# Two edits in a two-layer kernel: an empty interleaving step, and a table stored in one hop

## The reference, cut to what matters

```python
proj = h @ w_in[l]
(cb, cc, cv, q, k, v, qm, ga, gb, gc) = jnp.split(proj, IN_OFFSETS, axis=-1)
y_a = (cb * causal_dwconv(cc * cv, conv_mix_w[l])) @ w_conv_out[l]
o = moba_attention(to_heads(q), to_heads(k), to_heads(v), rel_bias)
y_b = jnp.transpose(o, (0, 2, 1, 3)).reshape(b_, s_, ATT_W) @ w_attn_out[l]
y_c = memory_attention(qm, rmsnorm(mem, g_mem[l]), w_mem_kv[l]) @ w_mem_out[l]

# in moba_attention, for the keys of a query's own block (and likewise for the earlier block):
s_own = jnp.einsum("bhqd,bhkd->bhqk", qc, ko).astype(jnp.float32) * scale
bias_own = bias_hb[:, rel_bucket(dist)]
s_own = jnp.where(dist[None, None] >= 0, s_own + bias_own[None], NEG)
```

## Time and profile before

| what | value |
|---|---|
| median of 3 runs | 2201.85 us (2200.92 to 2204.42) |
| profiled execution, its own time | 2201.85 us |
| its span (first to last instruction) | 2199.8 us |
| PE busy | 2022.4 us, 92% of the span |
| DVE, ACT, POOL busy | 993.9, 702.0, 218.5 us |
| chain that ended last | PE 70%, DMA 16%, DVE 8% |

### The profile page before, as it was taken

The page is one execution under the profiler, slowest core; times in us unless marked ns, Lnnn a source line. Parts: engine busy times, 40 slices in busy tenths (PEclk is TensorE's granted clock), DMA queues, the critical chain, the costliest instruction groups (busy, mean ns, idle before and its releaser), DMA issues.

```text
span 2199.8 us, 23022 instructions
## 1 busy us (share of the span) xinstructions
PE 2022.4 (92%) x9514; PEld 1407.9 (64%) x9514; DVE 993.9 (45%) x1558; ACT 702.0 (32%) x1122; POOL 218.5 (10%) x281
## 2 busy tenths in 40 slices
PE   7999999997999999889999999999995988888887
PEld 6767788896888788777777765666693332332232
DVE  4466524426666522677888436652235111111113
ACT  4343422324444312554555323552121110100100
POOL 2000000002000000001111002110023111111110
PEclk9999999998999999999999999999996999999999
DMA  7331122242222322232222221112229999999995
GB/s 259 106 112 61 67 87 96 97 153 105 97 96 96 134 96 86 100 136 90 74 96 101 87 95 58 58 58 77 77 106 376 414 423 423 424 422 422 417 411 225
DMA packets 56856, 380.43 MB, mean 173 GB/s; under 512 B 12936, under 2 KB 13192, under 8 KB 23856
## 3 DMA queue, kind: packets, MB, share of 16 engines
q1 hardware_dynamic: 38304, 339.23, 39.5%
q0 software_dynamic: 17872, 38.68, 5.0%
q10 hardware_dynamic: 576, 1.05, 0.1%
HBM read 378.82 MB, written 27.89 MB: 185 GB/s over the span
## 4 chain that ended last, share of the span: by engine, by line
PE 70%; DMA 16%; DVE 8%; ACT 3%; issue 1%; POOL 1%; SPq 0%; DVEq 0%; POOLq 0%; ACTq 0%
PE PS L490 17%; PE PS L491 16%; PE PS L492 16%; DMA AR<-in_wexp 15%; PE PS L1071 5%; PE PS L864 4%; PE PS L537 2%; DVE AR L1331 2%; DVE rf L1113 2%; ACT rf L1928 1%; PE PS L845 1%; PE PS L1094 1%; PE PS L486 1%; PE PS L897 1%; PE PS L929 1%
## 5 line engine op out<-in xcount | busy, mean ns | idle before, releaser
L490 PE MATMUL PS<-rf,rf 128*128 128x512 f32 (+1 forms) x1896 | 725.2, 382 | 22.9 <-DVE rf L1113 16.0
L491 PE MATMUL PS<-rf,rf 128*128 128x512 f32 (+1 forms) x1896 | 712.4, 376 | 0.0
L492 PE MATMUL PS<-rf,rf 128*128 128x512 f32 (+1 forms) x1896 | 711.5, 375 | 0.0
L1113 DVE TENSOR_TENSOR rf<-AR,rf 128x1024 fp32r<-128x1024 f32 (+1 forms) x210 | 268.4, 1285 | 385.1 <-ACT rf L1928 384.8
L490 PEld LDWEIGHTS PS<-rf,rf 128*128 128x128 f32 x1896 | 360.1, 190 | 97.6 <-issue 22.7
L492 PEld LDWEIGHTS PS<-rf,rf 128*128 128x128 f32 x1896 | 360.1, 190 | 64.8
L491 PEld LDWEIGHTS PS<-rf,rf 128*128 128x128 f32 x1896 | 360.3, 190 | 64.2 <-issue 3.1
L1928 ACT ACTIVATE rf<-AR 128x1024 fp32r<-128x1024 f32 (+1 forms) x210 | 229.1, 1101 | 304.4 <-PE PS L492 210.1
L1071 PE MATMUL PS<-AR 128*64 128x512 f32 x1024 | 271.7, 639 | 51.9 <-DMA AR<-in_wexp 50.8
L1071 PEld LDWEIGHTS PS<-AR 128*64 128x64 f32 x1024 | 84.2, 147 | 233.6 <-issue 159.8
L1873 DVE TENSOR_TENSOR AR<-AR,PS 128x256 f32<-128x256 f32 x32 | 13.5, 421 | 360.3 <-ACT AR L2370 360.3
(11 more groups left out here) (326 smaller groups left out, 1830.4 us busy)
## 6 DMA issues: line engine op xcount, KB each, us to landing
AR<-in_wexp SPq DMA_DIRECT2D x62, 2048.0 KB, 35.9
AR<-in_wpack SPq DMA_DIRECT2D x123, 1024.0 KB, 5.1
AR<-in_wexp SPq DMA_DIRECT2D x68, 1024.0 KB, 38.1
AR<-acud POOLq DMA_DIRECT2D x16, 512.0 KB, 4.1
AR<-ya SPq DMA_DIRECT2D x4, 1024.0 KB, 7.9
bvec<-bv POOLq DMA_DIRECT2D x1, 2560.0 KB, 16.3
AR<-in_x SPq DMA_DIRECT2D x4, 512.0 KB, 7.4
AR<-bvec POOLq DMA_DIRECT2D x8, 256.0 KB, 3.0
```

Of the source, the lines that this page charges most:

```text
L490: e.i.matmul(o, ws[0], xs[0], start=start, stop=False)
L491: e.i.matmul(o, ws[0], xs[1], start=False, stop=False)
L492: return e.i.matmul(o, ws[1], xs[0], start=False, stop=stop)
L1113: e.i.tensor_tensor(rounded(p.place + p.width, p.width), src, rounded(p.place, p.width).bitcast(F32), ALU.subtract).then_inc(*tick("w_lo", ...
```

## The change

There are two edits.

**1.** In `attention_1` of PE, DVE and ACT one of the two yields after the first pair of heads goes. All later steps of the attention then stand one dense step earlier among the dense work. POOL and SP have no such generators.

**2.** `bv8` goes, with its store and POOL's wait for it. One DMA now writes `bvec` straight from SBUF: its source is the 8 partitions of BV, each read 128 times, its destination `bvec` in order.

```diff
--- before.py
+++ after.py
@@ -601,7 +601,6 @@
 
 
                 scores(0)
-                yield
                 yield
                 for p in range(4):
                     if p < 3:
@@ -2421,10 +2418,8 @@
             for i in range(2):
                 norm(NM, i)
             e.wait_ge(*at("v_out", "bv"))
-            e.i.dma_start(dram["bv8"], BV[0:8, 0:640]).then_inc(*tick("bv8", 0, 16))
-            e.wait_ge(*at("bv8"))
-            e.i.dma_start(dram["bvec"].rearrange("h p c -> p h c"),
-                          dram["bv8"].unsqueeze(0).to_broadcast([128, 8, 640])).then_inc(*tick("bvec", 0, 16))
+            e.i.dma_start(dram["bvec"], BV[0:8, 0:640].unsqueeze(1).to_broadcast([8, 128, 640])).then_inc(
+                *tick("bvec", 0, 16))
             e.wait_ge(*at("acc", "bias"))
             e.i.dma_start(GB, dram["gains"][0:1, :].to_broadcast([128, 1024])).then_inc(*tick("gains", 0, 16))
             for h in range(8):
@@ -2896,7 +2891,7 @@
         a = _np.ascontiguousarray(a)
         ins[f"in_{name}"] = a
         dram[name] = nc.dram_tensor(f"in_{name}", a.shape, _mybir.dt.from_np(a.dtype), kind="ExternalInput").ap()
-    for name, shape, dt in (("bv8", [8, 640], F32), ("bvec", [8, 128, 640], F32), ("h2d", [512, 1024], F32),
+    for name, shape, dt in (("bvec", [8, 128, 640], F32), ("h2d", [512, 1024], F32),
                             ("x1d", [512, 1024], F32), ("x2d", [512, 1024], F32), ("tab", [128 * NOV, 1], I32),
                             ("ya", [1024, 1024], F32), ("acud", [16, 1024], F32)):
         dram[name] = nc.dram_tensor(name, shape, dt, kind="Internal").ap()
```

## The result

The changed kernel takes **2217.01 us** (median of four runs, 2216.34 to 2218.58) against 2201.85: a ratio of 1.0068, 95% interval 1.0050 to 1.0086. It is slower by 15.2 us. The forecast was 2203.4 with a range up to 2211.0, so the time lies outside the range. The profiled span goes from 2199.8 to 2214.9 us.

What follows compares the result with a forecast made beforehand. PE, busy in 92% of the span, was taken as the bound, so gains must come from its idle time or low clock. 2201.85 + 1.5 (edit 1) + 0 (edit 2) = 2203.4 us, range 2200.0 to 2211.0.

Steps and rivals of the forecast that it cites:

- Edit 1, +1.5 us: Attention start, 88 to 128 us: two old holes go, 9.2 us of idle time replace them; +1.5 us.
- the three pieces of idle time: PE idles from 104.7 to 107.1, 108.2 to 110.8 and 112 to 116.2, around the transposes and before mv: 9.2 us.
- the walk: New order walked with old durations: mv starts at 116.2 and ends at 128.8, where the V product follows.
- one stretch, 1.6 us: Clock down once more behind the last hole before mv, as behind the old 4.75 us hole: + 1.6 us.
- C: Rival: transposes amid the idle time before mv keep the clock at 1.00; 2201.8 us, chance 0.11.
- Weight loads that pass the copy get slower, but a full pipeline covers it. Cost 0: Weight loads beside the table copy: a load is due some 9 us later than its 5.1 us end; cost 0.
- My step on the table's time: Copy of bvec from 8 partitions at the old store's 56 GB/s: 47 us, landing at about 76.5, in time.
- My estimate of 33 us: Table copy split over at most 8 engines, so at half the old rate of all engines: 33 us.
- rival B: Copy takes longer than 58.7 us, so DVE's first maxima begin late; 2208.9 us, chance 0.23.
- Its own 62 us: Upper bound on the table copy: weight loads take their 0.24 DMA share; 62 us, landing at 91.5, 5.5 us late.
- D: Rival: dense work nearer the attention's waits fills the holes, 7 us would go; 2194.9 us, chance 0.06.

Runs made afterwards that it cites:

- E1: Edit 1 alone (one yield less) against the kernel before, the table by way of bv8 as before: 2204.0 us, ratio 1.0012.
- E6: The kernel before with the table copied in one hop from 16 neighbouring partitions (0 to 15), each written 64 times: 2214.12 us, ratio 1.0057.
- E7: The kernel before, two hops kept, but the second copy has 8 outermost rows, each read 128 times from DRAM: 2201.57 us, ratio 0.9999.
- E10: E6 with DVE's copy of q tile 3 and the mem norm's turning put ahead of the work on k's third part: 2200.52 us, ratio 0.9997.
- E5: The kernel before with the table copied in one hop from 8 spread partitions (0, 4, ..., 28): 2201.3 us, ratio 1.000.
- E3: The kernel before with one yield more in each of PE, DVE and ACT, so attention steps come later: 2193.32 us, ratio 0.9964.
- E4: Both edits, but the table stands on all 128 partitions, each written 8 times; against the kernel before: 2203.6 us, ratio 1.0011.

## Why the prediction was wrong

**Edit 1, +1.5 us: the mechanism was right, the size a little small.** The order of events, the three pieces of idle time and the start of mv (116.18) came as worked out; in the changed kernel mv starts at 130.60, the same point moved by the 14.4 us. By the profile ACT's copy of a transpose (L1989) ends the last wait and not DVE's L1139, but the two end within 0.1 us of each other (116.01 and 116.08). The waits are 2.37, 1.51 and 2.91 us, 6.8 us where the walk had 9.2, because the transposes between them take 2.16 and 2.37 us, together twice the 2.2 us I gave them: the granted clock is 0.56 from 107.2 to 109.4 and 0.50 until mv begins. That costs nothing, since the other engines set mv's start. What the walk had low is the clock behind it: I took one stretch, 1.6 us. In E1 the granted clock is 0.50 from 116.2 to 120 and 0.86 from 120 to 124,

```profile
116.20:120.00 3.80, 3.80 (x9) 3.03 (x10) 2.21 (x3) 0.75 (x1) 0.00 (x0) 0.50 0.82 280
120.00:124.00 4.00, 4.00 (x16) 3.22 (x16) 1.23 (x1) 1.06 (x1) 0.00 (x0) 0.86 0.58 227
```

which loses 3.8 x 0.50 + 4.0 x 0.14 = 2.5 us. That puts the V product at 129.57 instead of 128.8, and the term at 2.2 us by the trace. Timed it is 3.1 us, with an interval (0.7 to 4.8) that holds the 1.5 as well. C (the transposes keep the clock up) did not happen: the clock is down from the first of them on. Nothing was given back or lost from 130 us on: in E1 PE is busy for 311.90 of 312.00 us.

**Edit 2, "Weight loads that pass the copy get slower, but a full pipeline covers it. Cost 0": this step failed.** It has two halves.

*How much slower the loads get.* I bounded the table's time but not the loads'. They were to lose a share of the engines to a copy that moves 56 GB/s, little next to the 337 GB/s of the same stretch before. In fact every table packet holds its engine three to four times as long as before (0.78 against 0.24 us), and the load's packets queue behind it: 23 us for 1 MB. By the step's own number, a load may end 9 us later than its 5.1 us, so 23 us did not fit even by that. The kernel before had a sign of it that the median of 5.1 us in the earlier trace rows hides: one of the two loads beside its own 16.3 us copy took 10.4 us. My step on the table's time came near (47 us forecast, 55.8 measured), though its 56 GB/s are the starts of eight small packets; that these are set by the same thing as the long copy is not shown.

The Trainium skill, "SBUF — State Buffer" (the DMA port swizzle), gives one port to partitions 0 to 3; by that rule the estimate is 48 us for the two ports of 8 neighbours, measured 55.8 (47 GB/s), and 24 us for the four ports of E6, measured 29.0. "DMA: Bandwidth & Descriptors" (how many engines) in the Trainium skill splits 8 outermost rows over 8 engines at most. The trace agrees: where its copy runs almost alone, E7 takes 49.0% of the 16 engines at 209 GB/s (43 to 47 us), the kernel before all of them at 385 GB/s (34 to 38 us). My estimate of 33 us from it was still far too high, E7's copy took 19.9 us: I had doubled the 16.3 us of before, and much of these the copy spends beside weight loads, on engines it does not have to itself. The same page's advice to put a multiple of 16 outermost, followed in E6, brought the copy from 56.4 to 29.0 us and the kernel's loss only from 13.7 to 12.5 us.

*What the cover is.* Two finished parts of k, 5.4 us each, lie ahead of PE when it stops, and the load was needed by PE's matmuls only near 55 us. E10 shows that this just covers a load that comes at 52.7: PE begins the first part at 44.44 and so comes to the third at about 55.3, and its low (53.81, the first of two in 2.36 us) is ready at 55.0. But I counted the cover for the weights alone. DVE and ACT work in order, and behind the low and the high of that part stood the copy that empties a PSUM bank and the norm's turn, which PE needs at 45 us. So the load was late for whoever stood first behind it in the queue, at 45, not for its own reader at 55. In the kernel before:

```profile
39.04 1.23 DVE L1113 TENSOR_TENSOR rf<-AR,rf 128x1024 fp32r<-128x1024 f32 x1 [3.87 <-ACT rf L1928]
42.90 0.69 DVE L1140 COPY AR<-PS 128x512 f32<-128x512 f32 x1 [2.64 <-PE PS L492]
```

The low was over 2.6 us before the copy could begin. The load is issued near 29.4 (in E6 it comes at 52.7 after 23.3 us) and lands near 34.5 when it takes 5.1 us. From these rows I estimate the cover: 18 us to its own reader (52.7), but only 6 us to the bank's copy (42.9 less 1.0 for the high and 1.2 for the low). A load of 9.7 us fits (E5), one of 23 doesn't.

**The bias table comes late (rival B): did not happen.** The copy takes 55.8 us, more than the 47 of the estimate and less than the 58.7 of the bound; it ends 1.8 us in time. B had the right cause, the slow source, with the wrong victim. Its own 62 us (weights take their share) was too pessimistic: the 64 packets of 5120 bytes that each of 8 engines has to move are 50 us at 0.78 us each, so the weights cost the table some 6 us, and the table cost each load up to 20.

**D (the earlier attention fills the holes)** did not happen either; E3 shows that its 7 us were there, in the other direction.

## What to carry to other kernels

A DMA that is slow because of where it reads takes the engines from all others that run beside it. Don't judge it by its own due time and its bytes alone: look at what it does to the loads that share its time, and spread its source over partitions that don't lie side by side, or over all of them. And when a load may be late, its slack ends at the first instruction queued behind its consumer on an in-order engine that somebody waits for, not at the consumer's own reader: put copies that free banks ahead of work made in advance.

## What the runs showed of the hardware that I had not expected

- A busy share of the DMA engines says little of what they move when the source is slow: 97% busy at 111 GB/s (E6) against 95% at 355 GB/s when the same table is read from 128 partitions (E4).

```profile
30.00:45.00 15.00, 14.40 (x71) 11.91 (x69) 3.80 (x5) 1.66 (x2) 0.00 (x0) 1.00 0.97 111
```

```profile
30.00:45.00 15.00, 15.00 (x75) 12.61 (x74) 6.89 (x10) 3.77 (x6) 1.08 (x2) 1.00 0.95 355
```

- A table packet of 5120 bytes from neighbouring partitions takes 0.78 us of its engine, with 8 partitions on 8 engines as with 16 on 16; eight partitions four apart on 8 engines give about 0.20 us (E5, 43 to 47 us: 163 packets in 49.9% of the 16 engines' time).
- With 8 outermost rows about half the engines work, at about half the rate, 209 against 385 GB/s; yet the landing grows only from 16.3 to 19.9 us from DRAM (E7) and to 21.2 us from eight spread partitions (E5), because the copy with 128 outermost rows shares its engines with the weight loads for much of its time.
- An idle time of 11.1 us costs 2.45 us more through the clock behind it. In E1 a wait of 2.37 us was enough: the clock is down from 107.2 until past 120, through two more waits and the transposes between them, and 2.5 us of it cost time. In the kernel before, a wait of 2.25 us left it at 1.00 (107.6 to 111.1).
